# Two transformer blocks on one core: small TensorE products on all rows, fewer visits, and reordered vector work

## The reference

```
h = rms_norm(x); u, q, kv, nsa_g, merge_g = split(h @ w_in)
y = gate_pool * (pooling_mixer(u) @ w_pool_out) + gate_nsa * (nsa(q, kv, ...) @ w_nsa_out)
x = x + y @ w_out
gate_pre, val = split(rms_norm(x) @ w_up)
x = x + (silu(causal_dwconv(gate_pre)) * val) @ w_down
```

```
log_a = log_sigmoid(a_lr @ wa2 + ba) / 16           # a_lr has 16 columns
total = sum of log_a in the chunk; k_dec = k * exp(total - cumsum(log_a))
S_c = exp(total_c) * S_(c-1) + k_dec_c^T v_c        # state, per head 64 x 128
o_c = q_c S_c
```

## Time and profile before

| what | value |
|---|---|
| median of three runs | 1889.46 us (1889.43 to 1889.82) |
| the profiled execution's own time | 1889.91 us |
| its span, from the first to the last instruction | 1888.1 us |
| busy: PE | 1879.2 us (100%), 9689 matmul instructions |
| busy: weight loads of PE | 1545.5 us (82%) |
| a weight load of 128x128 | 187 to 188 ns (mean of the page's costliest groups) |
| busy: DVE | 1176.1 us (62%) |
| busy: ACT | 890.8 us (47%) |
| busy: POOL | 334.8 us (18%) |
| moved by DMA | 178.94 MB, mean 95 GB/s |
| granted clock of TensorE | 1.000 |

### The profile page before, as it was taken

The page is one execution under the profiler, slowest core; times in us unless marked ns, Lnnn a source line. Parts: engine busy times, 40 slices in busy tenths (PEclk is TensorE's granted clock), DMA queues, the critical chain, the costliest instruction groups (busy, mean ns, idle before and its releaser), DMA issues.

```text
span 1888.1 us, 25235 instructions
## 1 busy us (share of the span) xinstructions
PE 1879.2 (100%) x9689; PEld 1545.5 (82%) x9689; DVE 1176.1 (62%) x1950; ACT 890.8 (47%) x1431; POOL 334.8 (18%) x166
## 2 busy tenths in 40 slices
PE   9999999999999999999999999999999999999999
PEld 7977778788888888788888888888788888888887
DVE  7777547684553567797656745466589645755553
ACT  6564555543332445534445553445443444545442
POOL 1010012121120121343010110131235110010211
PEclk9999999999999999999999999999999999999999
DMA  6211114223222233132122123224222213122321
GB/s 240 96 68 68 46 46 156 90 89 112 89 93 107 89 134 134 68 109 92 45 106 74 67 92 112 90 94 151 90 90 89 89 46 112 48 91 89 134 90 68
DMA packets 26747, 178.94 MB, mean 95 GB/s; under 512 B 3088, under 2 KB 3984, under 8 KB 6416
## 3 DMA queue, kind: packets, MB, share of 16 engines
q1 hardware_dynamic: 24768, 164.11, 24.3%
q10 hardware_dynamic: 1872, 13.38, 1.9%
HBM read 171.19 MB, written 6.29 MB: 94 GB/s over the span
## 4 chain that ended last, share of the span: by engine, by line
PE 98%; DVE 1%; ACT 1%; DMA 0%; issue 0%; DVEq 0%; POOL 0%; ACTq 0%
PE pp L282 33%; PE pp L286 16%; PE pp L272 10%; PE pp L274 10%; PE pp L273 10%; PE po L282 4%; PE po L286 2%; PE po L928 1%; PE po L1213 1%; PE pt L894 1%; PE ps L1285 1%; PE ps L808 1%; PE po L1153 1%; PE pt L1177 0%; PE pt L1198 0%; PE ps L1233 0%
## 5 line engine op out<-in xcount | busy, mean ns | idle before, releaser
L266 DVE TENSOR_TENSOR wlo<-wraw,whi 128x2048 fp32r<-128x2048 f32 x123 | 286.2, 2327 | 234.7 <-ACT whi L261 234.0
L261 ACT ACTIVATE whi<-wraw 128x2048 fp32r<-128x2048 f32 x150 | 286.5, 1910 | 50.0 <-PE pp L286 49.9
L282 PE MATMUL pp<-hhi,whi 128*128 128x512 f32 (+1 forms) x693 | 279.6, 403 | 0.0
L282 PE MATMUL pp<-hlo,whi 128*128 128x512 f32 (+1 forms) x693 | 270.6, 390 | 0.0
L282 PE MATMUL pp<-whi,hhi 128*128 128x512 f32 x464 | 187.3, 404 | 0.0
L286 PE MATMUL pp<-hhi,wlo 128*128 128x512 f32 (+1 forms) x693 | 187.2, 390 | 0.0
L282 PE MATMUL pp<-whi,hlo 128*128 128x512 f32 x464 | 181.3, 391 | 0.0
L2028 POOL TENSOR_TENSOR wlo<-wraw,whi 128x2048 fp32r<-128x2048 f32 x26 | 120.7, 4643 | 230.1 <-ACT whi L261 230.1
L282 PEld LDWEIGHTS pp<-hhi,whi 128*128 128x128 f32 (+1 forms) x693 | 130.0, 188 | 32.2 <-issue 6.0
L286 PEld LDWEIGHTS pp<-hhi,wlo 128*128 128x128 f32 (+1 forms) x693 | 129.9, 187 | 28.1
L272 PE MATMUL pp<-split,whi 128*128 128x512 f32 x387 | 151.0, 390 | 0.0
(11 more groups left out here) (451 smaller groups left out, 3446.0 us busy)
## 6 DMA issues: line engine op xcount, KB each, us to landing
wraw<-weights SPq DMA_DIRECT2D x150, 1024.0 KB, 4.8
out_t<-xT ACTq DMA_DIRECT2D x4, 1024.0 KB, 3.9
xT<-out_t ACTq DMA_DIRECT2D x2, 2048.0 KB, 8.4
wraw<-weights SPq DMA_DIRECT2D x8, 256.0 KB, 6.6
work<-cmp_w ACTq DMA_DIRECT2D x1, 2048.0 KB, 8.9
xT<-x_t ACTq DMA_DIRECT2D x1, 2048.0 KB, 7.8
xT<-x_t SPq DMA_DIRECT2D x3, 512.0 KB, 8.4
out_t<-xT SPq DMA_DIRECT2D x3, 512.0 KB, 2.6
```

The lines of the kernel that those rows point to most:

```text
L261: nc.scalar.activation(whi[:, slot, :], wraw[:, slot, :], ACT.Copy).then_inc(w_hi, 1)
L266: nc.vector.tensor_tensor(wlo[:, slot, :], wraw[:, slot, :], whi[:, slot, :].bitcast(F32), ALU.subtract).then_inc(w_lo, 1)
L282: nc.tensor.matmul(out_ap, *pair, start=(start and n == 0 and part == 0), stop=False)
```

## The change

It has ten parts.

- Front: x slice 0 goes to ACT's queue, ahead of the vectors; only the first columns of the vectors (the mix gain) follow, the rest comes on SP's queue behind the front pieces. DVE copies the first weight piece to its high part itself (semaphore `w_zero`). PE's twelve products of slice 0 are ordered by what they need: high x high for tiles 0 and 1, then for 2 and 3, the low weights of tiles 0 and 1, the low part of `x` for all four, the low weights of 2 and 3. The lambda products move behind the sum of squares.
- `dve_window(1, 4)` is cut in two steps.
- merge1: the low part of the chunk that came after the first group of gated adds comes after two adds of the second.
- down rounds: the last two slices form the late group, not the last one.
- DSA: the scaling of the last row of a step comes before the next maximum.
- wout2: the first tile goes by `three` after a wait for `w_lo`.
- Gate product on 128 rows. POOL sets all rows of `alr_f` to one, not 32.
- Compressed V on 128 rows: for each head pair a zero-filled copy of `vc_f` with only its 32 rows, made by POOL (`vc_z`, semaphore `vz_in`), against all rows of `ct_f`.
- GLA: U products for four chunks at c = 0 and c = 4, O products at c = 4 (four chunks), 6 and 8 (two each), four state buffers. DVE does all eight state updates in a row, then the sums and conversions.
- Suffix sums: `la_f` is not scaled by 1/16 any more (the totals are, in ACT's exponential); DVE makes two fp32r parts of it, and PE sums them with an fp32r copy of `suf`, four products of 512 columns. The totals come first.

The diff, cut to its core:

```diff
@@ pe_fm
+                                if part is late[0] and m == 0 and name == "wout2":
+                                    pe.wait_ge(w_lo, c + 1)
+                                elif part is late[0] and m == 0:
-                                if part is late[0] and m == 0:
                ...
@@ compressed V
+                    pe.wait_ge(vz_in, 1)
                 for g in range(2):
-                    rows = slice(32 * t, 32 * t + 32)
-                    nc.tensor.matmul(po[g][y_rows(g), :], vc_f[rows, 64 * g:64 * g + 64], ct_f[g][rows, :], start=False,
+                    nc.tensor.matmul(po[g][y_rows(g), :], vc_z(t)[:, 64 * g:64 * g + 64], ct_f[g], start=False,
                                      stop=True).then_inc(o_done, 1)
@@ gate product
-                last = nc.tensor.matmul(pt[i // 2][:, 256 * (i % 2):256 * (i % 2) + 256], alr_f[0:17, i * P:i * P + P],
-                                        wa2_f[0:17, :], start=True, stop=True)
+                last = nc.tensor.matmul(pt[i // 2][:, 256 * (i % 2):256 * (i % 2) + 256], alr_f[:, i * P:i * P + P],
+                                        wa2_f, start=True, stop=True)
@@ suffix sums, PE
             pe.wait_ge(g_la, l + 1)
             pe.wait_ge(t_lo, tb + 12)
-            for i in range(QT):
-                nc.tensor.matmul(pt[i // 2][:, 256 * (i % 2):256 * (i % 2) + 256], suf, la_f[:, i, :], start=True,
-                                 stop=True)
...
+            pe.wait_ge(la_split, l + 1)
+            for y in range(2):
+                for x in range(2):
+                    last = nc.tensor.matmul(pt[x][:, :], sufr, la_r[y][:, 512 * x:512 * x + 512], start=(y == 0), stop=(y == 1))
@@ suffix sums, DVE
-            nc.vector.tensor_tensor(la_f, la_f, za_f, ALU.subtract)
-            dve.drain()
-            nc.vector.tensor_scalar(la_f, la_f, 1.0 / 16, None, ALU.mult).then_inc(g_la, 1)
+            nc.vector.tensor_tensor(la_f, la_f, za_f, ALU.subtract).then_inc(g_la, 1)
+            nc.vector.tensor_copy(sufr, suf)
+            dve.drain()
+            nc.vector.tensor_scalar(la_r[0], la, 1.0 / 16, None, ALU.mult)
+            dve.drain()
+            nc.vector.scalar_tensor_tensor(out=la_r[1], in0=la, scalar=1.0 / 16, in1=la_r[0].bitcast(F32), op0=ALU.mult,
+                                           op1=ALU.subtract).then_inc(la_split, 1)
@@ GLA, PE
+        GLA_OUT = {4: (0, 1, 2, 3), 6: (4, 5), 8: (6, 7)}
-                if c >= 2 and c % 2 == 0:
+                if c in GLA_OUT:
...
                 if c < 8:
-                    i = c // 2
-                    if c % 2 == 0:
-                        for hd in range(4):
+                    if c % 4 == 0:
+                        for i in range(c // 2, c // 2 + 2):
+                            for hd in range(4):
@@ GLA, DVE
-                if c == 6:
-                    dve_conv(dve, c0 + 2, slot0)
-                if c in (5, 7):
-                    dve_gla_sum(dve, l, (c - 5) // 2)
-            for i in range(2, QT):
+            dve_gla_sum(dve, l, 0)
+            dve_conv(dve, c0 + 2, slot0)
+            for i in range(1, QT):
                 dve_gla_sum(dve, l, i)
@@ DSA, DVE
+                    if s >= 1 and i == 0:
+                        dve_scale_row(dve, u0 + s - 1, s - 1, 3)
                     if s < 4:
                         dve_max(dve, u0 + s, i)
                     if s < 4 and i >= 1:
                         dve_scale_row(dve, u0 + s, s, i - 1)
-                    if s >= 1 and i == 0:
-                        dve_scale_row(dve, u0 + s - 1, s - 1, 3)
@@ front, PE
+            pe.wait_ge(w_zero, 1)
+            pe.wait_ge(xg_hi, 1)
+            for n in range(4):
+                if n == 2:
+                    pe.wait_ge(w_first, 1)
+                nc.tensor.matmul(banks[n][:, :], first[n][0], hhi[:, 0, :], start=True, stop=False)
+            pe.wait_ge(w_half, 1)
...
+            pe.wait_ge(xg_lo, 1)
...
+            pe.wait_ge(w_half, 2)
...
+            for x in range(1, 4):
@@ front, ACT
-            act.dma_start(vec[:, :], vec_in).then_inc(gain_in, 16)
+            act.dma_start(xT[:, 0:1, :], x_in[:, 0:1, :]).then_inc(x_in_sem[0], 16)
+            act.dma_start(vec[:, 0:V_FFN], vec_in[:, 0:V_FFN]).then_inc(gain_in, 16)
@@ front, DVE
+            dve.wait_ge(w_begun[0][0], 16)
+            nc.vector.tensor_copy(whi[:, 0, 0:512], wraw[:, 0, 0:512])
+            dve.drain().then_inc(w_zero, 1)
@@ down rounds
-                      lambda x: pe.wait_ge(ff_lo, FF[r] + x + 1), late=(range(ROUNDS[r] - 1), [ROUNDS[r] - 1]))
+                      lambda x: pe.wait_ge(ff_lo, FF[r] + x + 1), late=(range(ROUNDS[r] - 2), range(ROUNDS[r] - 2, ROUNDS[r])))
@@ window sums
-                        dve_window(dve, 1, 4)
+                        dve_window(dve, 1, 4, 1, 2)
+                    if s == 4 and i == 3:
+                        dve_window(dve, 1, 4, 2)
@@ merge1
+                    if k == 1 and m == 1:
+                        dve_conv(dve, c0 + 2, c0 % 2)
-                dve_conv(dve, c0 + k + 2, (c0 + k) % 2)
+                if k >= 1:
+                    dve_conv(dve, c0 + k + 2, (c0 + k) % 2)
@@ POOL, new
+            pool.wait_ge(kc_out, 2)
+            nc.gpsimd.memset(alr_f[:, 0:3 * P], 0.0)
+            nc.gpsimd.memset(vc_z(3), 0.0)
+            for t in range(4):
+                pool.drain()
+                rows = slice(32 * t, 32 * t + 32)
+                nc.gpsimd.tensor_copy(vc_z(t)[rows, :], vc_f[rows, :])
+            pool.drain().then_inc(vz_in, 1)
```

More of the change, by code:

```diff
@@ L1704, in act_layer @@
                         dst = a_f[rows, i, :].rearrange("p (h g d) -> p h g d", h=2, g=2)[:, :, g, :]
-                        last = nc.scalar.activation(dst, bank[rows, 0:256].rearrange("p (h d) -> p h d", h=2), ACT.Copy)
+                        last = nc.scalar.activation(dst, bank[rows, 256 * (i % 2):256 * (i % 2) + 256].rearrange("p (h d) -> p h d", h=2), ACT.Copy)
                     last.then_inc(go_out, 1)
@@ L2095, in front @@
                 return three(bank[:, :], (wh[:, x, cc], wl[:, x, cc]), (hhi[:, x, :], hlo[:, x, :]), x == 0, x == KT - 1)
-            for x in range(4):
+            banks = (po[0], po[1], pp[0], pp[1])
+            first = [[(w[:, 0, n % 2 * P:n % 2 * P + P]) for w in weights(n // 2, KT, 256)] for n in range(4)]
+            pe.wait_ge(w_zero, 1)
[5 more added lines that the diff above has]
+            pe.wait_ge(w_half, 1)
+            for n in range(2):
+                nc.tensor.matmul(banks[n][:, :], first[n][1], hhi[:, 0, :], start=False, stop=False)
+            pe.wait_ge(xg_lo, 1)
+            for n in range(4):
+                nc.tensor.matmul(banks[n][:, :], first[n][0], hlo[:, 0, :], start=False, stop=False)
+            pe.wait_ge(w_half, 2)
+            for n in range(2, 4):
+                nc.tensor.matmul(banks[n][:, :], first[n][1], hhi[:, 0, :], start=False, stop=False)
+            for x in range(1, 4):
                 pe.wait_ge(xg_lo, x + 1)
@@ L2263, in first_x @@
                 nc.scalar.activation(hhi[:, k, :], xT[:, k, :], ACT.Copy, scale=gain(0, k)).then_inc(xg_hi, 1)
-            for what, a, b in FRONT:
+            for what, a, b in FRONT[1:]:
                 if what == "w":
@@ L2570, in _ @@
                 if what == "w":
+                    if pieces > 0:
+                        dve.wait_ge(w_first, pieces)
                     pieces += 1
-                    dve.wait_ge(w_first, pieces)
                     cols = slice(512 * b, 512 * b + 512)
@@ L2585, in _ @@
             nc.vector.tensor_tensor(squares(0, 0), squares(0, 0), squares(0, 4), ALU.add).then_inc(sq_two, 1)
+            dve.wait_ge(vec_rest, 16)
+            for l in range(LAYERS):
+                for x in range(2):
+                    c = V_LAM + 4 * l + 2 * x
+                    nc.vector.tensor_tensor(lam[:, 2 * l + x:2 * l + x + 1], col(c), col(c + 1), ALU.mult)
+            dve.drain().then_inc(lam_in, 1)
             dve_conv(dve, 2, 0)
@@ L2861, in _ @@
         def _(sp):
-            for what, a, b in FRONT:
+            for what, a, b in FRONT[0:1] + FRONT[2:]:
                 if what == "w":
```

80 lines of the change are left out of this document (41 added, 39 removed).

## The result

The changed kernel takes 1879.69 us (median of five, 1879.39 to 1879.94) against 1889.46 (1889.41 to 1889.82): 9.77 us or 0.52% less, ratio 0.9947 with a 95% interval of 0.9935 to 0.9959. The forecast was 1880.8, with a range of 1877.5 to 1885.8.

A forecast was written before the change was run, and what follows sets the result against it. The prediction took TensorE (PE), busy practically all the time, to bound the kernel. Its ten terms summed to 8.65 us, so 1889.46 - 8.65 = 1880.8, with a range of 1877.5 to 1885.8.

The forecast's parts named there:

- What bounds the kernel: Whole kernel: PE is busy practically throughout, 98% of the chain; only less PE work or less PE waiting wins time.
- Idle plus 0.24 for a stop: PE's stops: each costs its shown idle time plus 0.24 us, read from start to start of products.
- down rounds: Three rounds: a second late x slice covers PE's wait for ACT's evacuation; saves 0.44 + 0.44 + 0.34 = 1.2, bounds 0 and 1.3.
- DSA: Two layers: scaling ahead of the next maximum readies rows for PE's transposes; 0.4 of 0.46 back twice, 0.8, bounds 0 and 1.3.
- Entry and exit: Gate, compressed V, GLA: entering and leaving another array configuration costs PE time; savings 0.68, 0.6 and 0.75.
- Compressed V's 0.05: Compressed V: allowance for a slower first product, estimated from the excess behind a stop; leaves 0.15 a visit, 0.6 for four.
- Suffix sums: Two layers: four fp32r passes replace eight fp32 ones; 0.5 to 0.6 a layer really won, 1.0 taken, bounds -1.0 and 2.0.
- Front: Kernel start: PE's first products start near 6.45 instead of 7.63 on high parts alone; 0.6 taken, bounds 0 and 1.2.
- Both cost nothing: Front: the moved lambda products' delay to DVE and SP's extra issue cost nothing; without cover, their own length, under 0.5.
- Second rival: Given back: PE's earlier starts are lost at the next tight waits; 1884.0, or 1885 to 1886; chance 0.14.
- Third rival: Slower: the front in pieces leaves PE at its low rate; 1894.4 for 60 products, 1902.6 for 96; chance 0.04.
- Fourth: Rival at the suffix sums: the parts come later than the small products end; 1882.8; chance 0.04.

## Why the prediction was right, point by point

*What bounds the kernel* was right, and with it the method: with PE at 98% of the chain, each tenth of a us that its starts move up is a tenth of the result.

*Idle plus 0.24 for a stop* held: window 0.71 for 0.76, merge 1 0.97 for 0.96, wout2 1.45 for 1.3. For the down rounds 1.35 came for 1.2, 0.04 too little for each place and above the bound of 1.3. For DSA 0.95 came for 0.8: the rule itself would have given 2 x (0.30 + 0.24) = 1.08, and the forecast had put less.

*Entry and exit* held at all three places (gate 0.82 for 0.68, just above its bound of 0.8), and the kernel with alternating rows shows it as a price for each change. Compressed V's 0.05 for a slower first product, an estimate by a likeness, came out (0.96 instead of 1.01).

*Suffix sums* is the step that failed: "soon after PE asks for the low weights, made by DVE until 1137.22 + 2.29 = 1139.51, asked for at 1140.15: only 0.64 early". The conversion that stood nearest to the demand in time was taken for the one demanded. It is the next chunk's. The rows alone could not tell, the code could. So the slack of 0.64 was none, nothing was given back, and the term is 2.00 in place of 1.0, at the very bound that was given for it. It accounts for 1.0 of the 1.4 by which the sum of the terms was too small. Of the others, the front came 0.25 short, and the down rounds, DSA, wout2 and the gate product each 0.14 or 0.15 over.

*Front* was near the measured sum by luck, through two errors. The start came at 7.11 and not at 6.45, since the short piece of the vectors was counted as landed and stood behind x slice 0 in its queue. PE then ran with less of a stop behind its first two products, so the lead of 0.55 was near the 0.7 that had been worked out. But one pair of profiles can't carry that number: with the old front the lead over the kernel before was 0.34 and 0.55 in two other profiles. "Both cost nothing" was wrong in the profiled execution: at the sums 0.2 were lost. In six of the seven other profiles with the same front the sums were in time, within 0.07, and over all profiles the front is worth some 0.4.

*Second rival.* Its size did not come, since nothing was given back, but one of its places was right: the slack at slice 7 is 0.3 in the changed kernel, and the kernel with the old front lost 0.4 there. The other named slacks gave nothing back. *Third rival:* the products of the front stood 0.23 apart from the start of slice 1 on, and the granted clock is 1.00 from 7 to 10 and from 10 to 30, so the rate was the full one, the level of 2.4 GHz; no run tried to bring the low one about. *Fourth:* the parts were there 0.2 before the sums started, the margin that the forecast put at about nothing.

## What to carry to other kernels

On an engine that is busy all the time, read start to start, and lay two traces beside each other matmul by matmul: edits of 0.3 to 2 us then come out one by one, most of them below what the medians can tell. The start of a kernel is the exception: where transfers land, two profiles of the same code can differ as much as the edit is worth, and only several profiles of each side tell. Put small products of another array configuration together, and fill up rows with zeros or ones where the columns stay: the rows are free, the change is not. Before a slack is priced, look up in the code which chunk a conversion makes; and keep more than half a us at a place that a gap on another engine can reach.

## What the runs showed of the hardware

A pair of changes, from the full array to a part of its rows and back, costs 0.39 to 0.44, so some 0.2 a change, for 17 rows as for 64. A stop of PE costs some 0.24 more than the idle time shown.

DVE has gaps of 0.42 to 0.49 that no wait explains, four to eight of them in each of the thirteen traces, 70 in all. They stand at the same instructions in kernels with the same DVE program (near 46, 193, 515, 817 and 1374 in the changed kernel and in that with three visits), and mostly elsewhere when four instructions are added. Counting every DVE instruction that a trace records, drains included, shows a pattern: ahead of the first loop they stand at number 64, 192, 321 or 448, and behind the last loop at 1256, 1384, 1896, 2024, 2152, 2280, 2408 or 2536, in some traces one later. Within each group these are whole multiples of 128 apart. (The one near 515 has number 852, between the loops.) It is the number that counts and not the instruction: in the changed kernel the gap near number 448 stands before a window sum (L2584), and with the five changes of order undone before a scaled row (L881).

The Trainium skill, Runtime: NRT & Kernel Launch, section Instruction fetch mechanics, says that an engine refills its instruction memory in blocks of 256 instructions and that the cost of crossing a block is mostly hidden. The page of the changed kernel has DMA queues of the kind "instruction"; this is one of them (packets, MB, share):

```profile
q14 instruction: 37, 0.30, 0.0%
```

Each of these packets has 8192 bytes, and though there are only 37 in a whole run, 66 of the 70 gaps are followed by one, 0.9 to 1.4 us after the gap begins. So the place and the time both speak for the refill, in blocks of 128 instructions on DVE and not of 256. Most crossings are hidden, as the Trainium skill says: the changed kernel has 2802 DVE instructions and five such gaps. What decides which crossing shows was not found, and no run took the refill away, so the cause is close to shown but not proven.

The landing of the front's pieces scatters: in the seven other profiles with the same front, PE's products of the first slices stood between 0.18 earlier and 0.23 later than in the changed kernel's, with no edit near them.
